# Latent attention: one fp32 product with a diagonal both turns and divides the probabilities

## The reference, cut to what matters

```
def causal_attention(q, k, v):              # 8 heads, q and k of 64 + 32 columns, v of 64
    scale = d ** -0.5
    for each block of 128 queries:
        sc = (qi @ k^T) * scale
        sc = where(mask, sc, float32.min)   # causal
        p = softmax(sc, axis=-1)
        out = p @ v
```

## Time and profile before

| what | value |
|---|---|
| device time, median of 3 runs | 4105.17 us (4099.12 to 4106.72) |
| the profiled execution | 4099.89 us, of which the profiled span is 4098.1 us |
| busy share of the span | PE 92%, PEld 71%, DVE 51%, ACT 26%, POOL 26% |
| mean granted TensorE clock | 0.952 of 2.4 GHz |
| first latent attention | from 2868.3 to 2941.3 us, 73.0 us; PE busy 57.3, DVE 30.0, ACT 26.4, POOL 34.4 us |
| second latent attention | from 3593.7 to 3667.6 us, 73.9 us; PE busy 58.3, DVE 30.0, ACT 26.4, POOL 34.4 us |

### The profile page before, as it was taken

One profiled execution on the slowest core, in us unless ns is written; L12 is line 12 of the kernel. 1 busy time (PEld: TensorE's weight loads), 2 busy tenths in 40 slices (PEclk: granted clock), 3 DMA queues, 4 the chain that ended last, 5 costly groups with the idle time before them and its releaser, 6 DMA issues. The chain is left out here.

```text
span 4098.1 us, 44475 instructions
## 1 busy us (share of the span) xinstructions
PE 3765.1 (92%) x16846; PEld 2898.0 (71%) x16846; DVE 2086.4 (51%) x2654; ACT 1073.3 (26%) x1473; POOL 1070.4 (26%) x835
## 2 busy tenths in 40 slices
PE   6889999778999979999898999897899999879999
PEld 5656888556788858887666888673578877347887
DVE  4445555775554575454445545565443345545334
ACT  2442222013221212222443222232321223332221
POOL 0342634610263416350342635001300000130000
PEclk9999999878999989999999999997899999889999
DMA  3114444211444324443112544210123322003332
GB/s 102 44 31 109 126 129 116 68 44 43 112 127 134 113 71 139 123 126 90 50 33 67 142 121 124 66 54 21 31 82 97 99 77 65 21 23 87 90 103 77
DMA packets 553376, 346.08 MB, mean 84 GB/s; under 512 B 32327, under 2 KB 534477, under 8 KB 553229
## 3 DMA queue, kind: packets, MB, share of 16 engines
q1 hardware_dynamic: 539404, 293.79, 25.5%
q0 software_dynamic: 13824, 50.34, 4.2%
HBM read 341.01 MB, written 3.08 MB: 84 GB/s over the span
## 5 line engine op out<-in xcount | busy, mean ns | idle before, releaser
L1259 PE MATMUL ps<-h_hi,w_hi 128*128 128x512 f32 x2880 | 1141.7, 396 | 33.0 <-DVE h_lo L2031 10.1
L1260 PE MATMUL ps<-h_lo,w_hi 128*128 128x512 f32 x2880 | 1126.1, 391 | 0.0
L1261 PE MATMUL ps<-h_hi,w_lo 128*128 128x512 f32 x2880 | 1125.7, 391 | 0.0
L1221 DVE TENSOR_TENSOR w_lo<-w,w_hi 128x2048 fp32r<-128x2048 f32 (+2 forms) x294 | 663.7, 2258 | 168.8 <-ACT w_hi L1214 166.3
L1214 ACT ACTIVATE w_hi<-w 128x2048 fp32r<-128x2048 f32 (+2 forms) x294 | 507.2, 1726 | 701.8 <-PE ps L1261 635.7
L1259 PEld LDWEIGHTS ps<-h_hi,w_hi 128*128 128x128 f32 x2880 | 544.2, 189 | 151.7 <-issue 35.4
L1261 PEld LDWEIGHTS ps<-h_hi,w_lo 128*128 128x128 f32 x2880 | 543.3, 189 | 115.2
L1260 PEld LDWEIGHTS ps<-h_lo,w_hi 128*128 128x128 f32 x2880 | 544.0, 189 | 108.4 <-issue 0.5
L1350 DVE TENSOR_TENSOR sg<-sg,ps 128x512 f32<-128x512 f32 x132 | 90.8, 688 | 719.4 <-ACT sg L1335 719.4
L1259 PE MATMUL ps<-a_hi,w_hi 128*128 128x512 f32 x1056 | 412.1, 390 | 0.0
L1261 PE MATMUL ps<-a_hi,w_lo 128*128 128x512 f32 x1056 | 411.0, 389 | 0.0
(11 more groups left out here) (445 smaller groups left out, 4137.9 us busy)
## 6 DMA issues: line engine op xcount, KB each, us to landing
w<-in_ffn_w_gate_up SPq DMA_DIRECT2D x176, 512.0 KB
w<-in_w_ada POOLq DMA_DIRECT2D x96, 512.0 KB, 6.9
w<-in_ffn_w_down SPq DMA_DIRECT2D x64, 704.0 KB
w<-in_w_gate_up SPq DMA_DIRECT2D x88, 512.0 KB
w<-in_w_down SPq DMA_DIRECT2D x32, 704.0 KB
w<-in_fox_w_in SPq DMA_DIRECT2D x32, 512.0 KB
w<-in_w_in SPq DMA_DIRECT2D x14, 1024.0 KB
w<-in_fox_w_in SPq DMA_DIRECT2D x8, 1024.0 KB
```

Of the source, the lines that this page charges most:

```text
L1221: last = nc.vector.tensor_tensor(lo, raw, hi.bitcast(F32), ALU.subtract)
L1259: nc.tensor.matmul(out, hi, a[0][:, k, :], start=k == 0, stop=False)
L1260: nc.tensor.matmul(out, hi, a[1][:, k, :], start=False, stop=False)
L1261: return nc.tensor.matmul(out, lo, a[0][:, k, :], start=False, stop=k == kt - 1)
```

## The change

In the latent attention alone, GpSimd's pass over the probabilities goes. The reciprocal is followed on VectorE by an instruction that multiplies a 128x128 identity by the 128 reciprocals, which gives a diagonal matrix; TensorE then multiplies each block of the probabilities, as the weights, by this diagonal as the moving operand, where it transposed the block before: (block)^T x diag(1/sum) is the turned and divided block. The forgetting attention of the first model keeps GpSimd and the transposes. The diagonals lie in `diag` for even heads and in `square` for odd ones, one 128x128 slice for each tile; before it overwrites a slice, VectorE waits for the turns of the head two before.

```
@@ FoxAttention.vector
         def reciprocal(i):
             s, t = divmod(i, ST)
             e.wait_ge(m.sem["exp_ready"], m.at("exp_ready", i + 1))
-            if s >= 2:
-                e.wait_ge(m.sem["p_scaled"], m.at("p_scaled", i - 7))
-            nc.vector.reciprocal(self.stat(self.ri, s, t), self.stat(self.rs, s, t)).then_inc(m.sem["sum_ready"], 1)
+            self.reciprocal(e, s, t)
...
@@ LatentAttention
+    def gpsimd(self, e): pass
+
+    def scales(self, s, t):
+
+        return (self.m.square[:, t * P:(t + 1) * P] if s % 2 else self.m.diag[:, t, :])
+
+    def reciprocal(self, e, s, t):
+        m = self.m
+        ri = self.stat(self.ri, s, t)
+        m.dve(e, m.nc.vector.reciprocal(ri, self.stat(self.rs, s, t)))
+        if s >= 2:
+            e.wait_ge(m.sem["p_turned"], m.at("p_turned", s - 1))
+        m.nc.vector.tensor_scalar(self.scales(s, t), m.c("ident"), ri, None, ALU.mult).then_inc(m.sem["p_scaled"], 1)
+
+    def turn(self, e, s, t):
+
+        m, i = self.m, ST * s + t
+        e.wait_ge(m.sem["p_scaled"], m.at("p_scaled", i + 1))
+        if t == 0 and s:
+            e.wait_ge(m.sem["pt_ready"], m.at("pt_ready", 3 * s))
+        for b in range(t + 1):
+            part, at = self.PT_AT[b][0], self.PT_AT[b][1] + (t - b) * P
+            last = m.nc.tensor.matmul(m.ps[:, 4 + part, at:at + P], self.pb[s % 2][t][:, b * P:(b + 1) * P], self.scales(s, t), start=True, stop=True)
+        if t == ST - 1:
+            last.then_inc(m.sem["p_turned"], 1)
```

More of the change, by code:

```diff
@@ L1931, in vector @@
         output(self.heads // 2 - 1)
+    def reciprocal(self, e, s, t):
+        m = self.m
+        if s >= 2:
+            e.wait_ge(m.sem["p_scaled"], m.at("p_scaled", ST * s + t - 7))
+        m.nc.vector.reciprocal(self.stat(self.ri, s, t), self.stat(self.rs, s, t)).then_inc(m.sem["sum_ready"], 1)
     def v(self, b, s):
@@ L1939, in end @@
         n = ST * h
-        finish(self.m, logits_ready=n, exp_ready=n, max_ready=n, sum_ready=n, p_scaled=n, p_turned=h, pt_ready=3 * h, pv_done=h, o_taken=h // 2)
+        finish(self.m, logits_ready=n, exp_ready=n, max_ready=n, sum_ready=n if self.n else 0, p_scaled=n, p_turned=h, pt_ready=3 * h, pv_done=h, o_taken=h // 2)
         if self.n:
```

## The result

The changed kernel took 4126.0 us (median of 7 runs, 4116.1 to 4135.8), the kernel before 4099.1 us beside it (7 runs, 4092.0 to 4106.7): a ratio of 1.0063, interval 1.0046 to 1.0080. It is slower, by some 27 us, with the forecast at 17. Measured twice more in the experiments, the ratio was 1.0026 (1.0014 to 1.0038) and 1.0066 (1.0044 to 1.0088), that is some 11 and 27 us. The second of the three lies outside the intervals of the other two, so the time alone does not give the cost to better than about 16 us. The profile does: it shows each latent attention by itself. (One of the twelve executions of the later kernel all_copies_early took 4912.5 us at a granted clock of 0.729; it is not in that kernel's ratio.)

A forecast was written before the change was run, and what follows sets the result against it. A loop of waits through VectorE's copies bounds the steady head; 4.75 + 1.92 + 0.64 + 1.21 = 8.52 us a layer, 17.0 in both, added to 4105.2 gives 4122.2 us, 0.42% slower. Range: 4112 to 4129 us.

The forecast's parts named there:

- What bounds the kernel: Steady heads of 7.77 us: no engine is full; a loop of waits through VectorE's copies sets the pace.
- Part 1, the removed pass: GpSimd's pass is off the path in steady heads; removing it gains 0.30 us at each layer's stage end.
- Part 2, the products: TensorE's turns: each block costs 0.113 us more, +0.68 us a head for six blocks, 4.75 us a layer.
- The rivals on the price: Product no dearer than transpose: 4110.5 us, chance 0.04; weight loads not overlapping, 0.19 us each: 4145 us, chance 0.03.
- Turn 3: Last tile's four blocks: +0.45 us, free because it lies in TensorE's 0.87 us of idle time.
- Part 3, the diagonal: VectorE's last diagonal delays the copies 0.32 us, 1.92 us a layer; late output copies add 0.64 us a layer.
- Part 4, the end: End of each stage: late copies and ten blocks on the path, less GpSimd's 0.30 us: +1.21 us.
- The first heads: Turns beside a later head cost +0.68 us; in the cold first head a later clock rise could add more.
- Sum: All terms over the latent attention stages: 8.52 us a layer, 17.0 us in both.
- The clock as a rival: Products wake the clock earlier in the stages, giving about 8.5 us back, 4113.7 us; chance 0.10.

The follow-up runs named there:

- all_copies_early: Kernel before with all three copies of the turned head early, VectorE's two and ScalarE's one: ratio to before 0.9980, both stages 135.3 us.
- no_pass: Kernel before without GpSimd's pass and nothing in its place, transposes kept, division by the sums left out: ratio to before 0.9989, both stages 144.5 us.
- the early copies: VectorE's two copies of the turned head moved ahead of the last reciprocal, output copy later: ratio to before 1.0027 on the changed kernel, 0.9990 on the kernel before.
- rounded_product: Changed kernel with probabilities and diagonals stored as fp32r, so the turning product is one record in place of two: ratio to before 1.0057.
- early_copies_before: Kernel before with VectorE's two copies of the turned head ahead of the last reciprocal and the output copy later: ratio to before 0.9990, both stages 139.7 us.
- diagonals_only: Changed kernel with the diagonals made on VectorE but unused, TensorE transposing as before, division left out: ratio to before 1.0038, both stages 159.1 us.
- diagonals_filled: Kernel with unused diagonals, transposes and no division, plus four idle bf16 products a head in TensorE's waits: ratio to before 1.0015, both stages 148.8 us.
- repeat_change: The changed kernel measured a second time without edit: ratio to before 1.0026, both stages 163.6 us.
- repeat_change_2: The changed kernel measured a third time without edit: ratio to before 1.0066, both stages 165.6 us.

## Why the prediction was right, point by point

- *What bounds the kernel.* Right. A loop of waits through the copies sets the pace; no_pass and the early copies show it, the latter from both kernels.
- *Part 1, the removed pass.* Right that it is off the path: no_pass gained 0.1 us as measured and some 0.5 without its one long head, for 0.6 forecast.
- *Part 2, the products.* The mechanism was right, and so was the price of a block: one more record, 0.11 us. What was left out is the 0.05 us at the start of each run of products. There are two runs in the loop, so a head paid 0.77 us in place of 0.68, some 0.6 us a stage. The 0.127 a record of the norm's product, which I had set aside as paced by its diagonals, is higher than any record here but the first of a run (0.111 to 0.112). The rivals on the price are out: the product has two records where the transpose has one, and at 0.11 us apart no weight load adds 0.19 us. Turn 3 fitted into the idle time as forecast.
- *Part 3, the diagonal.* Right: the copies start 0.31 us later behind the reciprocal, forecast 0.32. The output copy cost 0.25 us behind an odd head, forecast 0.32.
- *Part 4, the end.* From the last logits 1 to the end of the first stage the changed kernel took 18.4 us, the one before 16.0: 2.4 us, of which about 1.1 are the head's own. That leaves 1.3 us, forecast 1.21. In the second layer it was 18.4 against 16.1. The 0.30 us that the forecast took off in each layer for GpSimd was read in the first layer alone; in the second, no_pass gained 1.57 - 1.44 = 0.13 us there.
- *The first heads.* From the start of the stage to logits 1 of head 2 it was 1.4 us more in the first layer and 0.6 in the second. I had 0.68 from the products. The rest goes with the clock, which rose 14.5 and 16 us after the start in the kernel before and 15.7 us after it in both layers of the changed one.
- *Sum.* 17.0 us forecast, 18.7 in the first profile of the stages, 18.7 to 20.9 in three. The stages held 38.3 us at half clock in the first profile of the changed kernel and 37.3 in the one of the kernel before, so some 0.5 us of the 18.7 is the clock and the rest the added work.
- *The clock as a rival.* The one with a gain had the wrong sign, and I had weighed no loss beyond the ends. The products did not wake the clock; steady heads, which I had counted as safe at 1.00, lost 1.7 us each time that it fell, in three of six stages (in one of the three the end of the stage gave it back). The section of the Trainium skill that I weighed (TensorE: Matmul & The Clock Gate, Part 4 on the PE-mode transpose) says that a transpose does not count as busy for the clock in the same way. These runs do not bear that out as a difference between the two: a one-pass product of the same length in place of the transpose (rounded_product) let the clock fall at least as often and rise later. The two-record product was not tried at the busy time of a transpose.
- *The measured time.* That 4126.0 us came so near the forecast 4122.2 is luck in part. The kernel before took 4099.1 us beside it, not the 4105.2 that I had added to, so the difference was 27 us and not 17; measured again it was 11 and 27. The profiles place 18.7 to 20.9 us in the stages, and the rest in code that scatters with the granted clock. A part of that code may pay for the change; these runs can't exclude it, but they show no stretch of it that is longer with the change than in the other kernels.

## What to carry to other kernels

Before you relieve an engine, find what the others wait for: GpSimd's 34 us a stage were all cover, and moving its work to the two engines of the loop cost 19 us, while changing the order of copies in the loop gained 9 us with no work removed (both over the two stages). Where a row names a releaser, check when that engine's instruction ended; in early_copies_before the named engine had been done for 2 us and a copy on another was the wait. And read the granted clock of every variant before its waits: in diagonals_only the added waits cost 0.3 to 0.6 us a head by themselves and 1.7 us more a head by the clock. The same goes for a whole kernel that is measured more than once: compare the granted clock of the executions before you look for a cause in the code.

## What the runs showed of the hardware

- The granted clock fell from 2.4 to 1.2 GHz for 3.4 us once in each late head of diagonals_only (0.83 over 10 us), with no wait of TensorE longer than about 1 us before it, where the kernel before held 1.00 with the same instructions. Four idle bf16 products a head in the waits of diagonals_only held it at 1.00 through all steady heads (diagonals_filled; it fell at 2947.6 us, in the end of the first stage).
- With 128 columns of fp32 weights and 128 moving columns, TensorE's records start 0.11 us apart within a run at 2.4 GHz, whether they are transposes, rounded one-pass products or halves of true fp32 products. A run begins with more than that: 0.14 us to the second record for the rounded product and 0.163 for the true fp32 one (0.112 to 0.115 for transposes that wait for nothing). So three blocks took 0.33, 0.37 and 0.72 us: the rounded product costs nearly what a transpose does, the true one twice as much and 0.05 us a run.
- With 40 idle products ahead of a stage, 14 in its first wait and 9 in its last, the stage ran at 1.2 GHz for 3.4 us alone, within its first head, where it had been 17.9 and 15.8 us (all_copies_early). That took some 4.5 us off each stage (135.3 to 126.4 us for both).
- All executions of one kernel in one measurement can be granted a different clock than in another: 0.953 to 0.956 in repeat_change, 0.948 to 0.953 in repeat_change_2, with 4115.5 and 4130.3 us for the same kernel.
